# Section ends taken slab by slab, and gathered values turned ahead of the previous expert's down projection

## The reference

```python
def rmsnorm(x, g):
    xf = x.astype(jnp.float32)
    y = xf * lax.rsqrt(jnp.mean(xf * xf, axis=-1, keepdims=True) + EPS)
    return (y * g.astype(jnp.float32)).astype(x.dtype)

def adaln_in(x, g, m, i):
    return rmsnorm(x, g) * (1 + m[:, i, 1][:, None]) + m[:, i, 0][:, None]

def swiglu(h, w1, w3, w2):
    return (jax.nn.silu(h @ w1) * (h @ w3)) @ w2
...
        h = adaln_in(x, norm_g[l, 1], m, 1) @ w_in[l]
...
        x = x + m[:, 1, 2][:, None] * (mix @ w_out[l])
...
        h = rms_norm(x, norm_ffn_g[l]) * (1.0 + sc_f) + sh_f
        x = x + g_f * moe_ffn(h, w_router[l], b_router[l], w1[l], w3[l], w2[l], ws1[l], ws3[l], ws2[l])
```

## Time and profile before

| | |
|---|---|
| median of 3 runs | 3786.5 us (3773.27 to 3791.08) |
| the profiled execution's own time | 3798.87 us |
| its span, mean granted TensorE clock | 3796.9 us, 0.964 of full speed |
| PE matmul busy | 3530.8 us, 93% of the span |
| PE weight load busy | 2989.7 us, 79% |
| DVE, ACT, POOL busy | 2332.1 us, 1477.7 us, 240.3 us |
| HBM read | 836.37 MB, 221 GB/s over the span |

### The profile page before, as it was taken

One profiled execution on the slowest core, in us unless ns is written; L12 is line 12 of the kernel. 1 busy time (PEld: TensorE's weight loads), 2 busy tenths in 40 slices (PEclk: granted clock), 3 DMA queues, 4 the chain that ended last, 5 costly groups with the idle time before them and its releaser, 6 DMA issues.

```text
span 3796.9 us, 52579 instructions
## 1 busy us (share of the span) xinstructions
PE 3530.8 (93%) x21065; PEld 2989.7 (79%) x21065; DVE 2332.1 (61%) x3517; ACT 1477.7 (39%) x2212; POOL 240.3 (6%) x337
## 2 busy tenths in 40 slices
PE   4999899999899998889999999999988999999999
PEld 2997799997699787789767676778778976766776
DVE  6774475775377474546666666656554766666666
ACT  1432233432143204133555555541232355555554
POOL 3010010010001000000000000000000000000000
PEclk9999899999899899889999999999998999999999
DMA  7785286784178552345889998875432688898986
GB/s 260 250 297 165 81 293 196 244 293 152 57 245 303 187 188 100 122 153 183 271 283 292 293 286 283 279 239 171 134 121 90 214 273 270 284 289 274 296 274 191
DMA packets 580320, 842.63 MB, mean 222 GB/s; under 512 B 22715, under 2 KB 489760, under 8 KB 578832
## 3 DMA queue, kind: packets, MB, share of 16 engines
q1 hardware_dynamic: 514508, 665.85, 53.5%
q0 software_dynamic: 41056, 147.35, 11.8%
q10 hardware_dynamic: 24548, 26.57, 2.8%
HBM read 836.37 MB, written 3.33 MB: 221 GB/s over the span
## 4 chain that ended last, share of the span: by engine, by line
PE 77%; DVE 9%; DMA 7%; ACT 3%; issue 2%; SPq 1%; DVEq 0%; ACTq 0%
PE bank L990 14%; PE bank L895 11%; PE bank L896 11%; PE bank L897 11%; PE bank L1336 8%; DMA ring<-in_w 3%; DMA far_up<-in_w 3%; PE bank L1349 2%; PE bank L1306 2%; PE bank L1307 2%; PE bank L1203 2%; PE bank L890 2%; PE bank L1301 2%; PE bank L1303 1%; PE bank L1302 1%
## 5 line engine op out<-in xcount | busy, mean ns | idle before, releaser
L897 PE MATMUL bank<-hh,ring_lo 128*128 128x256 f32 (+1 forms) x2176 | 621.7, 286 | 0.0
L895 PE MATMUL bank<-hh,hi 128*128 128x256 f32 (+1 forms) x1984 | 570.8, 288 | 16.7 <-issue 12.3
L896 PE MATMUL bank<-h_lo,hi 128*128 128x256 f32 (+1 forms) x1984 | 567.0, 286 | 0.0
L990 PE MATMUL bank<-h,ring 128*128 128x256 f32 x2432 | 556.4, 389 | 8.4 <-ACT h L1513 8.4
L990 PEld LDWEIGHTS bank<-h,ring 128*128 128x128 f32 x2432 | 475.7, 196 | 80.2 <-issue 12.1
L897 PEld LDWEIGHTS bank<-hh,ring_lo 128*128 128x128 f32 (+1 forms) x2176 | 419.9, 193 | 0.0
L895 PEld LDWEIGHTS bank<-hh,hi 128*128 128x128 f32 (+1 forms) x1984 | 382.7, 193 | 25.3 <-issue 17.6
L896 PEld LDWEIGHTS bank<-h_lo,hi 128*128 128x128 f32 (+1 forms) x1984 | 382.9, 193 | 0.5 <-issue 0.5
L895 PE MATMUL bank<-hid,hi 128*128 128x256 f32 (+1 forms) x1216 | 346.8, 285 | 2.2 <-DVE ring_lo L2592 2.2
L896 PE MATMUL bank<-hid_lo,hi 128*128 128x256 f32 (+1 forms) x1216 | 343.9, 283 | 0.0
L897 PE MATMUL bank<-hid,ring_lo 128*128 128x256 f32 (+1 forms) x1088 | 307.6, 283 | 0.0
(11 more groups left out here) (372 smaller groups left out, 6642.6 us busy)
## 6 DMA issues: line engine op xcount, KB each, us to landing
ring<-in_w SPq DMA_DIRECT2D x258, 1024.0 KB, 12.3
ring<-in_ffn_w SPq DMA_DIRECT2D x120, 1024.0 KB, 10.5
wmod<-in_w_mod POOLq DMA_DIRECT2D x216, 512.0 KB, 5.6
far_up<-in_w SPq DMA_DIRECT2D x84, 1024.0 KB, 13.1
ring<-in_w_in SPq DMA_DIRECT2D x74, 1024.0 KB, 6.0
work<-in_w SPq DMA_DIRECT2D x42, 1024.0 KB
ring<-in_w_out SPq DMA_DIRECT2D x16, 1024.0 KB, 5.1
ring<-in_w_mod SPq DMA_DIRECT2D x12, 1024.0 KB, 12.7
```

The source lines that it names most:

```text
L895: pe.matmul(o, w_hi, x_hi, start=start, stop=False, skip_group_check=True)
L896: pe.matmul(o, w_hi, x_lo, start=False, stop=False, skip_group_check=True)
L897: return pe.matmul(o, w_lo, x_hi, start=False, stop=stop, skip_group_check=True)
L990: ins = pe.matmul(o[:, half * T:(half + 1) * T], l_, r_, start=(k == 0), stop=(k == KD - 1))
```

## The change

At a mixer's end `next_halves` and `add_out` give way to `end_mixer` on ACT and DVE: the table of the root is loaded first, then one up slab of the next section is split, slabs 0 to 3 are added and squared, the other up slabs are split, and slabs 4 to 7 follow. PE takes the norm's first four slabs between the third and the fourth block of the last projection. The first down slab of an ffn is split behind the norm (`first_halves(sec, 2)`), that of a mixture still in `end_mixer`. At the joint of sections 2 and 3 ACT no longer waits for `down_done` ahead of the up splits. DVE calls `take_mods` ahead of its wait for the root in sections 2, 5 and 9. `more_setup` stands behind the norm of section 1, and the load of the masks moves from section 6 to section 1, where `x` need not be waited for. In the mixture, `turn_few(n)` stands ahead of `finish(n - 1)` on PE, `turned_few(n)` ahead of `out_hi(n - 1)` on ACT and its DVE half ahead of `out_lo(n - 1)`; `hidden_few` has two buffers for it, and `turn_few` waits for `hid_done` of the turn before.

```diff
         pre = nc.alloc_sbuf_tensor_at("pre", [P, 2 * T], F32, offset=place["macc"] + 4 * 2 * D)
-        hidden_few = nc.alloc_sbuf_tensor_at("hidden_few", [P, T], F32, offset=place["macc"] + 4 * (2 * D + 2 * T))
+        hidden_few = [nc.alloc_sbuf_tensor_at("hidden_few", [P, T], F32, offset=place["macc"] + 4 * (2 * D + 2 * T)), work[:, 64, :]]
         product = nc.alloc_sbuf_tensor_at("product", [P, T], F32, offset=place["macc"] + 4 * (2 * D + 3 * T))
         picks = rounded("picks", [P, 4, 4, P], "wmod")
...
@@ -869,12 +869,13 @@
                         ins = pe.matmul(bank[2 + f % 2][:, :], dft[:, r, f * P:(f + 1) * P], fk[:, r, :], start=(r == 0), stop=(r == 3))
                     ins.then_inc(f_mm, 1)
 
-            def norm(s):
-
-                for k in range(KD):
+            def norm(s, parts=range(KD)):
+
+                for k in parts:
                     pe.wait_ge(sq_done, KD * s + k + 1)
                     ins = pe.matmul(bank[2][:, 0:T], M["ones"], sq[:, (k + 4) % KD, :], start=(k == 0), stop=(k == KD - 1))
-                ins.then_inc(ms_done, 1)
+                if KD - 1 in parts:
+                    ins.then_inc(ms_done, 1)
 
             def sum_mods(n):
 
...
                     linear(slabs[9 + c], 9 + c, taken0, heads=att)
+                    if c == 2:
+                        norm(s + 1, range(4))
 
             def long_conv(X, taken0):
 
...
 
                 def turn_few(n):
                     p, wide = GATHER_NO[n], ORDER[n][0] == "wide"
+                    pe.wait_ge(hid_done, t0 + 2 * n)
                     if wide:
                         pe.wait_ge(product_done, g0 + p + 1)
                         for c in range(2):
...
                             scatter(n - 2)
+                        turn_few(n)
                         finish(n - 1)
-                        turn_few(n)
                     else:
                         up_dense(n, 0)
                         if gathers(n - 1) and gathers(n - 2):
...
                 act.wait_ge(red_done, 1 + 2 * DEPTH)
                 act.activation(lsum, lsum, ACT.Exp).then_inc(lam_exp, 1)
 
+            def squares(s, parts):
+                for k in parts:
+                    act.wait_ge(x_done, KD * s + k + 1)
+
+                    act.activation(sq[:, (k + 4) % KD, :], x[:, k, :], ACT.Square).then_inc(sq_done, 1)
+
             def norm(sec):
                 s = sec["s"]
                 if s == 0:
                     act.wait_ge(turned, KD + 1)
 
-                act.activation(idle, eps, ACT.Sqrt)
-                for k in range(KD):
-                    act.wait_ge(x_done, KD * s + k + 1)
-
-                    act.activation(sq[:, (k + 4) % KD, :], x[:, k, :], ACT.Square).then_inc(sq_done, 1)
+                if not sec["behind_mixer"]:
+                    act.activation(idle, eps, ACT.Sqrt)
+                    squares(s, range(KD))
                 split = sec["kind"] in ("ffn", "moe")
                 if split and not sec["early"]:
...
                     act.activation(h[:, k, :], h[:, k, :], ACT.Identity, bias=shift).then_inc(h_ready, 1)
+                if sec["kind"] == "ffn" and sec["early"]:
+                    first_halves(sec, 2)
 
             def split_up(slots, t, count=None, m=P):
 
 
-                for j in range(2):
+                for j in range(len(slots[0:2])):
                     if count is not None:
                         act.wait_ge(full[slots[j]], count(j))
                     act.activation(up_hi(j, t, m), up_half(slots[j], t, m), ACT.Copy).then_inc(hi_done, 1)
...
                     split_down(slots[2], 0, None, counts[2], m)
 
-            def next_halves(sec):
-                if sec["s"] + 1 < SECTIONS:
-                    first_halves(plan[sec["s"] + 1])
+            def end_mixer(sec):
+
+                nxt = plan[sec["s"] + 1]
+                s, m = nxt["s"], REST_T if nxt["kind"] == "ffn" else P
+                slots, counts = [q[0] for q in nxt["slabs"][0]], [q[1] for q in nxt["slabs"][0]]
+                act.activation(idle, eps, ACT.Sqrt)
+                split_up(slots[0:1], 0, lambda j: counts[0], m)
+                squares(s, range(4))
+                act.wait_ge(full[slots[1]], counts[1])
+                act.activation(up_hi(1, 0, m), up_half(slots[1], 0, m), ACT.Copy).then_inc(hi_done, 1)
+                first_halves(nxt, 1)
+                if nxt["kind"] == "moe":
+                    first_halves(nxt, 2)
+                squares(s, range(4, KD))
 
...
                     silu_tile(1, tile + 3)
                     if last and joined(sec["s"]):
-                        act.wait_ge(down_done, tile + 3)
                         first_halves(plan[sec["s"] + 1], 1)
                     if not last:
...
                     if slots(n) == WIDE:
-                        act.activation(hidden_few[:, :], bank[1][:, 0:T], ACT.Copy).then_inc(hid_done, 2)
+                        act.activation(hidden_few[GATHER_NO[n] % 2][:, :], bank[1][:, 0:T], ACT.Copy).then_inc(hid_done, 2)
                     else:
                         act.activation(product[:, 0:P], bank[1][:, 0:P], ACT.Silu).then_inc(product_done, 1)
...
                         middle(n)
                         columns_hi(n + 1)
                         split_ups(n + 1, 1)
+                        turned_few(n)
                         out_hi(n - 1)
-                        turned_few(n)
...
-                if s == 6:
-                    act.wait_ge(x_done, KD * (s + 1))
-                    act.dma_start(masks.rearrange("p a t -> p (a t)"), A["k_causal"]).then_inc(masks_in, 16)
                 norm(sec)
                 if s == 1:
+                    more_setup()
                     load_bias()
+                    act.dma_start(masks.rearrange("p a t -> p (a t)"), A["k_causal"]).then_inc(masks_in, 16)
                 if s == 6:
                     act.wait_ge(red_done, 1 + 2 * DEPTH + 1)
                     then(act.activation(trig[:, 0, :], trig[:, 1, :], ACT.Abs))
...
                     first_halves(sec)
+                if s in (2, 5, 9):
+                    take_mods(s)
                 dve.wait_ge(std_done, s + 1)
                 dve.reciprocal(rstd[:, :], std[:, :]).then_inc(rstd_done, 1)
-                if s not in (7, 8):
+                if s not in (2, 5, 7, 8, 9):
                     take_mods(s)
                 dve.wait_ge(rstd_done, s + 1)
                 for k in range(KD):
@@ -2049,10 +2071,8 @@
                         lo_h(sec, k - 1)
                 if sec["kind"] == "ffn":
                     lo_h(sec, KD - 1)
-
-            def next_halves(sec):
-                if sec["s"] + 1 < SECTIONS:
-                    first_halves(plan[sec["s"] + 1])
+                    if sec["early"]:
+                        first_halves(sec, 2)
...
@@ -2276,14 +2297,28 @@
                         then(dve.scalar_tensor_tensor(out=work[:, SQ1 + t, :], in0=U[:, 4 + t, :], scalar=col("d_skip", t),
                                                       in1=bank[4 + t // 2][:, (t % 2) * T:(t % 2 + 1) * T], op0=ALU.mult, op1=ALU.add))
                         dve.tensor_tensor(h[:, 4 + t, :], work[:, SQ1 + t, :], U[:, t, :], ALU.mult).then_inc(X["conv"], 1)
-                next_halves(sec)
-                add_out(sec, 9)
-
-            def add_out(sec, j):
-                for c in range(4):
+                end_mixer(sec, 9)
+
+            def end_mixer(sec, j):
+
+                nxt = plan[sec["s"] + 1]
+                m, slots, counts = REST_T if nxt["kind"] == "ffn" else P, [q[0] for q in nxt["slabs"][0]], first_counts(nxt)
+
+                def add_out(c):
                     dve.wait_ge(proj_done, sec["proj0"] + j + c + 1)
-                    for m in range(2):
-                        add_to_x(sec["s"], 2 * c + m, bank[4 + (j + c) % 4][:, m * T:(m + 1) * T])
+                    for half in range(2):
+                        add_to_x(sec["s"], 2 * c + half, bank[4 + (j + c) % 4][:, half * T:(half + 1) * T])
+
+                lo_up(slots[0:1], 0, lambda i: counts[0][0], m)
+                add_out(0)
+                add_out(1)
+                dve.wait_ge(hi_done, counts[0][1])
+                dve.tensor_tensor(up_half(slots[1], 0, m, ring_lo), up_half(slots[1], 0, m), up_hi(1, 0, m), ALU.subtract).then_inc(lo_done, 1)
+                first_halves(nxt, 1)
+                if nxt["kind"] == "moe":
+                    first_halves(nxt, 2)
+                add_out(2)
+                add_out(3)
 
             def tables():
...
@@ -2642,11 +2676,11 @@
                             dve.tensor_tensor(product[:, :], pre[:, 0:T], bank[0][:, T:2 * T], ALU.mult).then_inc(product_done, 1)
                         columns_lo(n + 1)
                         lo_ups(n + 1, 1)
-                        out_lo(n - 1)
                         spread_slots(n)
                         if slots(n) == NARROW:
                             dve.wait_ge(product_done, g0 + p + 1)
```

(3 more changed lines are left out.)

33 lines of the change are left out of this document (17 added, 16 removed).

## The result

| | before | after |
|---|---|---|
| median | 3786.5 us (3773.27 to 3791.64, 5 runs) | 3745.12 us (3742.72 to 3750.88, 5 runs) |
| profiled run's span | 3796.9 us | 3743.3 us |
| mean granted clock | 0.964 | 0.970 |

The ratio is 0.9905, with a 95% interval of 0.9885 to 0.9924: 0.95% faster, some 36 us, which from 3786.5 us gives 3750.5 us. On another chip the same kernel gave 0.9912 (0.9892 to 0.9932). It is near the time of rival 1 (3750 us), not near the likeliest time (3778.5 us).

What follows compares the result with a forecast made beforehand. PE was taken as the bound (77% of the chain that ended last), with DMA near full in the mixtures. Section ends gaining 14.0 us less 6 lost at gathered experts gave 8 us: 3778.5 us, range 3750 to 3798.

Steps and rivals of the forecast that it cites:

- rival 1: Turns fill PE's waits in the gathered experts: 22.3 us gained there, 36.3 with the section ends, 3750 us; chance 0.27.
- Section 0 into 1: With `more_setup` behind the norm, the table load is early, the norm takes 3.62 us without idle time: 5.36 us gained.
- section 5 into 6: ACT no longer waits for x to load the masks before its table load; norm ends earlier: 5.18 us gained.
- 2 into 3: Down split and wait for `down_done` go from ahead of the table load: 1.99 us gained.
- rival 3: Section ends give half, through PE's low clock after idle gaps or slower steps of the squares: 3785.5 us; chance 0.11.
- Mixer ends into an ffn: At 1 into 2 and 4 into 5, root 0.87 us sooner and `take_mods` 0.48 us: 1.35 us gained each.
- Mixer ends into a mixture: At 6 into 7 and 8 into 9, nothing waited before; the new tail is bare: 1.2 us lost in all.
- Rival 4: In two of six changed ends PE was the bound already; counted in the sum as a loss, no separate chance.
- Sum of the section ends: All changed section ends together: 5.36 + 5.18 + 1.99 + 2.70 − 1.2 = 14.0 us gained.
- Table load: An ACT table load takes 1.28 us with nothing behind it, against about 2.66 us by the Trainium skill's page.
- Gathered experts: Turn ahead of the down projection in the mixtures: bounds 31.3 us gained and 36 us lost; 6 us lost taken.
- two counter-costs: Across 18 runs of gathered experts, turns held 1.0 us for `pre` and weight-slab releases 1.0 us later: 18 us each.

## Why the prediction was right and where it was wrong

- *Section 0 into 1, 5.36 us:* the norm came out as said (3.62 us, no idle time); the end gave 3.55. The step that failed is "`sum_mods` moves with it": it moved, but took 7.73 us for 5.92, at a granted clock of 0.68 in place of 0.90. At section 5 into 6 it was 5.80 for 5.18, at 2 into 3 only 0.89 for 1.99. Of the two causes that rival 3 had for the slow norm of before, the rows show the low clock (0.71), not a slower step of the squares; what the forecast counted as gained there was in part only moved behind the norm.
- *Mixer ends into an ffn, 1.35 us each:* 1.62 and 1.82. The root's tail, 1.53 + 1.07 us, was 448.89 − 446.54 = 2.35, so the root stood 4.1 us behind the end of the last projection's own work, for the 4.5 forecast.
- *Mixer ends into a mixture, a loss of 1.2 us for both:* 0.43 + 0.26. The sign was right; a part of a change can lose where PE was the bound. Rival 4 speaks of two of six changed ends; there are seven.
- *Sum of the section ends, 14.0 us:* 13.0 at the places themselves, 24.6 (16 to 33) by whole runs of that half alone, of which 13.9 ± 4 at full clock. The mechanism is right and so is the sum. The other 12 us are clock, for which the forecast had no term.
- *Table load:* 1.28 us with nothing behind it also after the change, so the sum by the rows was the better one:

```profile
279.17 1.28 ACT L1508 ACT_TABLE_LOAD   x1
280.46 0.20 ACT L1508 ACTIVATE small<-small 128x1 f32<-128x1 f32 x1
```

  The Trainium skill's drain (page "ScalarE: Activation LUTs", section "What ACT_TABLE_LOAD costs") is not seen in any run here: in each trace 19 to 23 of the 38 or 39 loads are followed by the next activation within 0.1 us.
- *Gathered experts, 6 us lost:* this is the step that failed. The forecast chose between +31.3 and −36 by the row "DMA 0.89 and ACT waiting for it", and took it that "fills return nothing since the weight stream sets the pace". Measured: 20.9 us gained by the turns alone (interval 13 to 28), 26.5 by those inside a run; at full clock and by the spans 12 to 13 and 18 to 22. Rival 1 had 22.3, by the mechanism that the runs show but with other parts: the waits for `hg` fell by 36.1 us, for which it had 31.3, and 16.3 us of waits came new at the turns, for which it had 9. The forecast's two counter-costs, 18 us for late releases and 18 for held turns, came to those 16.3 us of waits in all, and in the run with the borders alone to 3.4 ± 3 us at full clock. The prediction's own sign for rival 1, runs shorter by over a microsecond each, was met only by the turns inside a run (1.1 us; 0.6 for the changed kernel). The stream had room: the same 836.37 MB were read in less time, and ACT's waits for the experts' weights from 1780 on grew, from 93.5 us in all to 131.4, while the run became shorter. Their largest row, section ends only (turn behind), then the changed kernel:

```profile
ACT hi_far L1798 <- DMA ring<-in_w: 32.6, 13, 10.2
```

```profile
ACT hi_far L1791 <- DMA ring<-in_w: 53.3, 24, 10.3
```

  So part of PE's saved time is now spent by ACT in waiting for slabs, and PE hardly waits for that.
- *The fill itself* goes as worked out. At the place that answers to the earlier trace rows the turn now stands in the wait, and what is left of 1.72 us is 0.74:

```profile
2026.68 1.08 PE L1325 MATMUL bank<-sort,pre 128*128 128x64 f32 x8
2028.49 3.62 PE L1342 MATMUL bank<-work,hidden_few 128*64 128x512 f32 x8 [0.74 <-DVE hg L2640]
```

- *The whole:* the sign was right and the likeliest time, 3778.5 us, was 28 us too high by the ratio and 33 by the median. The range reaches down to the result only because it was drawn to take in rival 1, and by the ratio it holds it with 0.5 us to spare: that is luck. So is the agreement with rival 1's 36.3 us. Its parts are 22.3 + 14.0 = 36.3; the changed kernel shows 23.8 us (± 7) at full clock and 9.4 (± 6) by the clock, for which no term stands. The 50.9 us of labelled waits spoke for a gain at the turns, and the gain was given 0.27.

## What to carry to other kernels

A wait with a name and a sum (here 50.9 us for one tile) is better evidence than the utilisation of a second resource: 0.89 busy is not a bound until the waits for it stand on the engine that sets the end. When an instruction goes ahead of another, look slot by slot for where there is a wait to fill, and turn the order only there. Before a last projection that PE leaves without waiting, splitting a reduction in two costs more than it hides (0.7 us for both places here, by the rows). When a group of instructions is slow, look at its granted clock before it is put down to a wait; and when whole runs gain more than the changed places do, count the runs at full clock first.
